# One transfer for the gate and up weights of pairs 7 to 30, and a new order of work in the first two pairs of a mixture-of-experts pass

## The reference

```python
for l in range(DEPTH):                       # DEPTH = 2
    mix = hybrid_mixer(x, mem, w_in[l], ...)
    x = layer_norm(DEEPNORM_ALPHA * x + mix, ln1_g[l], ln1_b[l])
    ffn = moe_ffn(x, w_router[l], router_bias[l], w_gate[l], w_up[l], w_down[l],
                  ws_gate[l], ws_up[l], ws_down[l])
    x = layer_norm(DEEPNORM_ALPHA * x + ffn, ln2_g[l], ln2_b[l])

def swiglu(x, wg, wu, wd):
    return (jax.nn.silu(x @ wg) * (x @ wu)) @ wd
# moe_ffn: sum over a token's 8 experts of weight * swiglu(x, w_gate[e], w_up[e], w_down[e])
#          + swiglu(x, ws_gate, ws_up, ws_down)   (the shared expert)
```

## Time and profile before

| what | value |
|---|---|
| median of 3 runs | 1187.55 us (1187.35 to 1188.29) |
| the profiled execution's own time | 1188.19 us |
| its span, first to last instruction | 1186.4 us |
| PE busy | 1148.7 us, 97% |
| DVE, ACT busy | 352.7 us, 255.3 us |
| moved by DMA | 456.49 MB, mean 385 GB/s |
| chain that ended last | PE 76%, DMA 21%, DVE 2% |
| mean granted TensorE clock | 0.996 |

### The profile page before, as it was taken

The page is one execution under the profiler, slowest core; times in us unless marked ns, Lnnn a source line. Parts: engine busy times, 40 slices in busy tenths (PEclk is TensorE's granted clock), DMA queues, the critical chain, the costliest instruction groups (busy, mean ns, idle before and its releaser), DMA issues.

```text
span 1186.4 us, 15935 instructions
## 1 busy us (share of the span) xinstructions
PE 1148.7 (97%) x6752; PEld 523.0 (44%) x6752; DVE 352.7 (30%) x1053; ACT 255.3 (22%) x511; POOL 8.4 (1%) x20
## 2 busy tenths in 40 slices
PE   8999999999999999999999999999999999999995
PEld 7774633433343333333386655333343334333331
DVE  0424722222222222222333346232222222222224
ACT  1132421222122211111112323221222122112111
POOL 0000000000000000000000000000000000000001
PEclk9999999999999999999999999999999999999998
DMA  9982599999999999999998626999999999999995
GB/s 378 421 328 113 213 415 425 428 427 426 428 426 427 428 427 428 427 427 428 413 425 360 252 80 254 412 428 428 426 429 426 428 427 426 429 426 428 426 425 224
DMA packets 39952, 456.49 MB, mean 385 GB/s; under 512 B 4416, under 2 KB 4544, under 8 KB 8256
## 3 DMA queue, kind: packets, MB, share of 16 engines
q1 hardware_dynamic: 39872, 455.38, 91.5%
HBM read 452.22 MB, written 3.15 MB: 384 GB/s over the span
## 4 chain that ended last, share of the span: by engine, by line
PE 76%; DMA 21%; DVE 2%; issue 0%; ACT 0%; POOL 0%; POOLq 0%; DVEq 0%
PE bank L705 29%; DMA slots<-in_w_gu 20%; PE bank L725 14%; PE bank L926 5%; PE bank L854 5%; PE bank L607 4%; PE bank L634 4%; PE bank L863 2%; PE bank L1052 2%; PE bank L825 1%; PE bank L713 1%; PE bank L829 1%; PE bank L873 1%; PE bank L883 1%; PE bank L959 1%; PE bank L619 1%
## 5 line engine op out<-in xcount | busy, mean ns | idle before, releaser
L705 PE MATMUL bank<-slots,front 128*64 128x512 f32 x2048 | 456.0, 595 | 13.6 <-DMA slots<-in_w_gu 13.5
L705 PEld LDWEIGHTS bank<-slots,front 128*64 128x64 f32 x2048 | 139.9, 137 | 280.8 <-issue 249.4
L725 PE MATMUL bank<-slots,r 128*32 128x512 f32 x2016 | 229.9, 595 | 1.1 <-issue 1.1
L1403 DVE SCALAR_TENSOR_TENSOR yparts<-bank,small,yparts 128x512 fp32r<-128x512 f32 x128 | 96.0, 750 | 265.4 <-ACT yparts L1086 265.4
L1086 ACT ACTIVATE yparts<-bank,small 128x512 fp32r<-128x512 f32 x128 | 87.9, 687 | 239.8 <-PE bank L725 239.8
L1395 DVE TENSOR_TENSOR high<-high,bank 128x256 f32<-128x256 f32 x64 | 26.9, 421 | 354.5 <-ACT high L1113 326.7
L725 PEld LDWEIGHTS bank<-slots,r 128*32 128x32 f32 x2016 | 59.3, 109 | 137.2 <-issue 135.7
L1113 ACT ACTIVATE high<-bank 128x256 f32<-128x256 f32 x60 | 23.0, 384 | 413.1 <-PE bank L705 413.1
L1086 ACT ACTIVATE front<-bank 128x512 f32<-128x512 f32 (+1 forms) x161 | 84.5, 580 | 88.7 <-PE bank L825 28.2
L607 PEld LDWEIGHTS bank<-selr,xparts 128*128 128x128 f32 x512 | 64.3, 188 | 45.4 <-issue 45.4
L634 PE MATMUL bank<-yparts 64*128 64x512 f32 x512 | 79.4, 421 | 1.9 <-DVE yparts L1403 1.9
(11 more groups left out here) (123 smaller groups left out, 616.6 us busy)
## 6 DMA issues: line engine op xcount, KB each, us to landing
slots<-in_w_gu SPq DMA_DIRECT2D x116, 2048.0 KB, 30.8
slots<-in_w_dn SPq DMA_DIRECT2D x58, 2048.0 KB, 27.5
slots<-in_dense SPq DMA_DIRECT2D x28, 1024.0 KB, 14.8
slots<-in_w_gu SPq DMA_DIRECT2D x24, 1024.0 KB, 9.0
slots<-in_w_dn SPq DMA_DIRECT2D x10, 1024.0 KB, 37.4
slots<-in_first SPq DMA_DIRECT2D x3, 768.0 KB, 7.0
r<-in_pool_mat SPq DMA_DIRECT2D x2, 1024.0 KB, 25.9
sdn<-in_shared_dn SPq DMA_DIRECT2D x2, 1024.0 KB, 10.0
```

The source lines that it names most:

```text
L705: m = pe.matmul(H[64 * a:64 * a + 64, :], cells[:, cell(B, k, j), a, :], GU[g][:, a, :, k, :], start=k == 0, stop=k == KD - 1)
L725: m = pe.matmul(Y[half][r0:r0 + 32, :], hT[:, kc * P + 64 * a + 32 * t:kc * P + 64 * a + 32 * t + 32], wd[:, a, kc, :], start=kc == 0, sto ...
L1403: dve.scalar_tensor_tensor(ysp[:, 1, half * 512:(half + 1) * 512], Y[half][:, :], wslot[:, b:b + 1], ysp[:, 0, half * 512:(half + 1) * 512 ...
```

## The change

There are four edits.

1. SP loads gate and up of pairs 6 to 29 in one transfer of 4 MB, issued when the pair three before has done its whole gate_up. PE waits for it before the first matmul of gate_up.
2. SP loads the first MB of pair 2's second half as soon as the first four k chunks of the second token tile's shared gate and up are read (`sgu_rd`), then half of pair 3's down weights into `xs`, then the last MB when `sh1` is full.
3. PE, ACT and DVE get a written-out order for pairs 0 and 1: gate_up of pair 1 comes before down of pair 0. On SP gate and up of pairs 3 and 4 are issued before the down weights of 3 and 4.
4. `shared_down` runs in pairs 14 to 17 and not in 26 to 29.

The diff, cut to its core:

```diff
 SPLIT = 3
+SHARED = PAIRS // 2 - 2
+WHOLE = range(6, PAIRS - 2)
+HALVES = [[q for q in range(g, PAIRS, 3) if q not in WHOLE] for g in range(3)]
...
-                def body(n, q, g, b, use, first, last):
+                def gates(n, q, g):
                     if round_ is None and q < 6:
                         for h, half in ((0, ps.h_half), (1, ps.h_full)):
                             a, m, z = h * W_CHUNK, h * W_CHUNK + W_CHUNK // 2, (h + 1) * W_CHUNK
...
+                    elif round_ is None and q in WHOLE:
+                        sp.wait_ge(ps.h_full, n - 2)
+                        sp.dma_start(slots[:, g, 0:2 * W_CHUNK], w_gu[l * PAIRS + q]).then_inc(ps.w_in[1][g], 16)
                     else:
                         sp.wait_ge(ps.h_half, n - 2)
                         load_gu(ps, l, q, g, (0,))
                         sp.wait_ge(ps.h_full, n - 2)
                         load_gu(ps, l, q, g, (1,))
+
+                def body(n, q, g, b, use, first, last):
+                    gates(n, q, g)
                     sp.wait_ge(ps.y_full, 2 * (n - 2))
                     load_dn(ps, l, q, g)
-                pairs_of_pass(base, body, 3, (lambda: load_count(sp, l)) if round_ is None else None)
+                if round_ is None:
+                    gates(base + 3, 3, 0)
+                    gates(base + 4, 4, 1)
+                    for q in (3, 4):
+                        sp.wait_ge(ps.y_full, 2 * (base + q - 2))
+                        load_dn(ps, l, q, q % 3)
+                pairs_of_pass(base, body, 5 if round_ is None else 3, (lambda: load_count(sp, l)) if round_ is None else None)
...
                 sp.dma_start(spill, xs[:].rearrange("p t d -> p (t d)")).then_inc(spill_out, 16)
-                sp.wait_ge(*full_at(l, "sh1"))
-                load_gu(main, l, 2, 2, (1,))
+                a, m, z = W_CHUNK, W_CHUNK + W_CHUNK // 2, 2 * W_CHUNK
+                sp.wait_ge(sgu_rd, l + 1)
+                sp.dma_start(slots[:, 2, a:m], w_gu[l * PAIRS + 2][:, a:m]).then_inc(third_in, 16)
                 sp.wait_ge(split_rd, 2 * l + 2)
                 sp.wait_ge(*full_at(l, "xTb3"))
                 sp.wait_ge(spill_out, 16 * l + 16)
                 sp.dma_start(xs[:].rearrange("p t d -> p (t d)"), w_dn[l * PAIRS + SPLIT][:, 0:KF * D]).then_inc(ahead_in, 16)
+                sp.wait_ge(*full_at(l, "sh1"))
+                sp.dma_start(slots[:, 2, m:z], w_gu[l * PAIRS + 2][:, m:z]).then_inc(main.w_in[1][2], 16)
...
                         if k % 4 == 0:
+                            if round_ is None and q == 2 and k:
+                                pe.wait_ge(third_in, 16 * l + 16)
                             if round_ is None and 3 <= q < 6:
                                 pe.wait_ge(quarter_in[g][k // 4], 16 * l + 16)
-                            pe.wait_ge(ps.w_in[k // 4][g], (turn * USES[g] + use) * 16 + 16)
+                            if k or (round_ is None and q in WHOLE):
+                                pe.wait_ge(ps.w_in[1][g], (turn * USES[g] + use) * 16 + 16)
+                            elif round_ is None:
+                                pe.wait_ge(ps.w_in[0][g], (turn * len(HALVES[g]) + HALVES[g].index(q)) * 16 + 16)
+                            else:
+                                pe.wait_ge(ps.w_in[0][g], (turn * USES[g] + use) * 16 + 16)
                         for a in range(2):
...
                         turn_sel(ps, q + 1)
-                        if round_ is None and q >= PAIRS - 6:
-                            i = q - (PAIRS - 6)
+                        if round_ is None and SHARED <= q < SHARED + 4:
+                            i = q - SHARED
                             shared_down(l, i // 2, i % 2)
+
+                def first_two():
+
+                    pe.wait_ge(ps.sel_rd, first_block + 2)
+                    gate_up(base, 0, 0, 0, True)
+                    for i in range(2):
+                        gather(ps, i, Y[i])
+                    shared_turn(l, 1)
+                    turn_h(base)
+                    pe.wait_ge(ps.selT_sb, base + 1)
+                    turn_sel(ps, 1)
+                    gate_up(base + 1, 1, 1, 0, False)
+                    for n, q in ((base, 0), (base + 1, 1)):
+                        if q:
+                            turn_h(n)
+                            for i in range(2):
+                                pe.wait_ge(ps.lo_rd, 2 * n - 1 + i)
+                                gather(ps, 2 + i, Y[i])
+                            combine(ps, base, 0, 0, l)
+                            combine(ps, base, 0, 1, l)
+                        pe.wait_ge(ps.w_in[2][q], turn * USES[q] * 16 + 16)
+                        pe.wait_ge(ps.hT_sb, n + 1)
+                        for half in range(2):
+                            pe.wait_ge(ps.g_sb, first_fill + KD + 2 * q + half + 1)
+                            down(q, q, half)
+                    pe.wait_ge(ps.selT_sb, base + 2)
+                    turn_sel(ps, 2)
...
-                pairs_of_pass(base, body, 0, (lambda: load_count(pe, l)) if round_ is None else None)
+                if round_ is None:
+                    first_two()
+                pairs_of_pass(base, body, 2 if round_ is None else 0, (lambda: load_count(pe, l)) if round_ is None else None)
...
                                       start=k == 0, stop=k == KD - 1)
                     if ks[-1] == KD - 1:
                         filled(l, f"sh{t}", m)
+                    elif t == 1:
+                        m.then_inc(sgu_rd, 1)
...
+                if round_ is None:
+                    for q in range(2):
+                        act.wait_ge(ps.h_full, base + q + 1)
+                        act.activation(sg[:, 0, :], H[:, 0:F], ACT.Silu).then_inc(ps.silu_rd, 1)
+                        if q:
+                            hi(base, 0)
+                        for i in range(2):
+                            g_out(1, 2 * q + i, Y[i])
+                        if q == 0:
+                            shared_turned(l, 1)
+                    hi(base + 1, 1)
+                pairs_of_pass(base, body, 2 if round_ is None else 0, (lambda: load_count(act, l)) if round_ is None else None)
...
+                if round_ is None:
+                    dve.wait_ge(ps.g_full, KD * (turn * BLOCKS + 1))
+                    build_sel(1)
+                    gated(base)
+                    turned(base)
+                    take_selT(base + 1, 1)
+                    gated(base + 1)
+                    dve.wait_ge(ps.selT_sb, base + 1)
+                    if l:
+                        dve.wait_ge(ps.lo_rd, 2 * base)
+                    lo(base, 0, 0)
+                    lo(base, 0, 1)
+                    turned(base + 1)
+                    dve.wait_ge(ps.selT_sb, base + 2)
+                    dve.wait_ge(ps.lo_rd, 2 * base + 2)
+                    lo(base + 1, 1, 0)
+                    lo(base + 1, 1, 1)
+                    take_selT(base + 2, 0)
+                pairs_of_pass(base, body, 2 if round_ is None else 0, (lambda: load_count(dve, l)) if round_ is None else None)
```

4 lines of the change are left out of this document (2 added, 2 removed).

## The result

The changed kernel takes 1192.73 us (median of 6 runs, 1190.84 to 1195.20), the kernel before 1187.92 us beside it (6 runs, 1187.35 to 1189.16): ratio 1.0044, 95% interval 1.0033 to 1.0054. It is 4.8 us slower. The forecast was 1190.5 us, 3.0 us slower than the 1187.55 that it started from. The measured time lies in the whole range of 1185.6 to 1194.0 us and 0.2 us above the 1189 to 1192.5 that the forecast's own case had. The profiled execution of the change took 1192.73 us with a span of 1190.9, so its span is 4.5 us longer than that of before. (The title counts pairs from 1: its pairs 7 to 30 are the pairs q = 6 to 29 of the text, whose gate and up go in one transfer.)

What follows compares the result with a forecast made beforehand. A pass ends by the DMA stream's length, start and losses, plus PE work behind the last landings. Per layer 1.8 - 1.6 + 1.3 = 1.5 us later, two layers 3.0: 1187.55 + 3.0 = 1190.5 us, range 1185.6 to 1194.0.

Steps and rivals of the forecast that it cites:

- the forecast's own case: Whole kernel: the summed terms hold, 1190.5 us within 1189 to 1192.5; chance 0.53.
- Edit 3, PE's part: Pairs 0 and 1: PE waits 1.9 us and 0.6 us more, entering gate_up of pair 2 some 2.5 us late.
- Edit 3, the stream's part: Opening, to pair 6's landing: late issues into empty queues make the DMA stream 1.8 us late per layer.
- Edit 2: Pair 2's early MB: worth at most 2.5 us of earlier stream per layer, used up by two empty queues.
- Edit 1, the transfer: Pairs 7 to 29: merged loads save 0.07 us a pair, 1.6 us per layer.
- the first rival: Merged loads: engines cut rows at 16 KB, so merging brings nothing; 1193.7 us; chance 0.12.
- Edit 1, the tail: Pair 29: PE must wait for all 4 MB, so the tail ends 1.3 us later per layer.
- the third rival: Tail: pair 29's gate and up land early enough, so the tail costs nothing; 1188.0 us; chance 0.2.
- Edit 4: Pairs 14 to 17: shared products, 7.6 us of PE, move no landing; PE meets the stream at pair 26.
- The second rival: Opening: the early MB's gain stays and the stream never runs dry; 1182.0 us; chance 0.13, half-way cases included.
- The fourth: Rival on merged loads: they save more than their rows show, the stream gets ahead of PE; 1178.6 us; chance 0.02.

Runs made afterwards that it cites:

- x2: The change with only the wait for the second selection matrix moved back behind gate_up of pair 0; 1190.48 us, ratio 1.0023.
- x9: The kernel before with only the early load of the first MB of pair 2's second half; 1190.54 us, ratio 1.0023.
- x4: The change with no merged 4 MB loads, halves of 2 MB from pair 6 on; 1193.84 us, ratio 1.0045.
- x6: The kernel before with only the new order for pairs 0 and 1 and SP's list to match; 1194.05 us, ratio 1.0052.
- x12: The whole change with matmuls of unused result filling PE's waits for pairs 0 and 25 to 29; 1192.48 us, ratio 1.0040.
- x11: The kernel before with merged loads for pairs 6 to 29, shared products in pairs 14 to 17, two unused matmuls ahead of pair 29's gate_up; 1186.47 us, ratio 0.9990.
- x5: The kernel before with merged loads for pairs 6 to 28 and shared products in pairs 14 to 17, pair 29 in halves; 1185.39 us, ratio 0.9980.
- x10: The kernel before with merged loads for pairs 6 to 29 and shared products in pairs 14 to 17; 1187.27 us, ratio 1.0003.
- x7: The kernel before with only the shared products moved to pairs 14 to 17; 1187.08 us, ratio 0.9999.
- x8: The kernel before with only merged loads for pairs 6 to 29, shared products still in pairs 26 to 29; 1192.06 us, ratio 1.0040.
- x3: The change with merged loads for pairs 6 to 28 only, pair 29 in two halves; 1192.69 us, ratio 1.0037.

## Why the prediction was right, and where it was not

**Edit 3, PE's part: right.** 1.76 and 0.68 us of waits for 1.9 and 0.6, gate_up of pair 2 2.7 us late for 2.5. x2 shows that the first of the two is what the stream pays for.

**Edit 3, the stream's part: this step failed in size.** "The stream is 1.5 to 2.1 us late here; I take 1.8." Down of pair 4 landed at the forecast time, but pair 6 at 211.4 instead of 209.4 to 210.0, and at down of pair 8 the stream is 2.7 and 3.3 us late. That is 2.4 us too little over both passes, where the whole sum was 1.8 us too low. The step charged the lateness of issues and the empty queue up to down of pair 4, and then took pair 6's transfer as if only its own length lay ahead of it. What failed is this sentence on pair 6: "At 7.2 to 7.8 us for the first 2 MB plus 4.9 for the others, they land at 209.4 to 210.0." It lets the load start when it is issued, at 197.36, but down of pair 5 lay ahead of it (issued at 190.28, 10.2 us to its landing) and moved until 200.4 us. Behind that landing pair 6 took 11.0 us in the first pass and 11.4 in the second, where 4 MB in a full queue take 9.7. It was issued 3.1 and 2.9 us before that landing, in the stretch of lead that x9 found dear.

Merging pair 6 brought this about. A 4 MB load goes out only when the whole slot is free, 3.5 us later than a first half would. In the ten passes with pair 6 in halves its first half was issued 6.2 us or more before the landing ahead of it and took 4.9 us, the step of a full queue. In the 18 passes with pair 6 in one transfer the lead was 2.8 to 5.1 us, and the load took 9.7 to 12.1 us, 0.7 us more than in a full queue on average: 0.9 with the opening of edit 3 and 0.6 with the old one. The kernel with edit 3 and pair 6 in halves, but pairs 7 to 29 merged, was not tried. Whether the late opening itself costs more beside merged loads stays open too: the shortest runs of x4 and x6, without them, say 1.9 to 2.0 us a pass, near the 1.8, while x12 against x11, both with them and with fillers, differ by 6.0 us, 3.0 a pass.

**Edit 2: right in its sum, wrong alone.** It was priced at nothing to 2.5 us of gain per layer, "used up by the two empty queues". Within the change that holds as far as x4 (edits 2, 3 and 4) against x6 (edit 3) shows: 1193.84 and 1194.05 us, with the same lag in their first passes. Alone it costs 0.7 to 2.1 us a pass (x9): the bytes moved earlier shorten the queue behind them.

**Edit 1, the transfer: right.** Landings of down weights in the undisturbed middle are 14.61 us apart, before 14.69: 0.08 us a pair for a forecast of 0.07, and from down of pair 8 to the last load the change wins 1.6 and 1.5 us for 1.6. In x5, which merges one pair less, it is 1.4 us a pass in the trace and 1.2 in the median. Rows of 32 KB stay whole, so the first rival is out, although its 1193.7 us is nearer to the measured time than the forecast's 1190.5; the page counts fewer packets for the same bytes:

```profile
DMA packets 33327, 456.48 MB, mean 383 GB/s; under 512 B 3680, under 2 KB 3808, under 8 KB 7520
```

against 39952 before; halving the number of rows in 48 loads of 4 MB takes 48 x 128 = 6144 away, and the trace holds 6144 packets of 32 KB, where that of before has none over 16 KB. The Trainium skill (DMA: Bandwidth & Descriptors, Why a DMA increments its semaphore by 16 and not by 1) names only rows longer than 64 KiB as ones to be cut. For rows of 32 KB the count of packets agrees.

**Edit 1, the tail: right in kind, too high in size.** 1.1 and 0.7 us in the change, 1.0 in x10's pass without a fall, 0.9 and 0.0 in x11, 0.9 and 0.3 in x12, for 1.3; x11 and x5 differ by 1.1 us for both passes together. This error offsets a part of the opening's: with the change's own 1.1 and 0.7 in place of 1.3 the forecast would have been 0.8 us lower and so farther off. That it came within 2.2 us of the median is in part luck. The wait at pair 29 is there (2.13 us), so the third rival is out.

**Edit 4: right.** No landing moved, PE meets the stream at pair 25 in the first pass and 24 in the second (forecast 26), and alone it is worth nothing that the runs can tell (x7). The forecast took it off the tail's pair before it added edit 1's wait; x8 shows what that is worth, 3.0 us a pass from the last load to the end instead of about 1.

**The second rival,** by which the early MB stays, was to be decided by down of pair 4 landing below 183.2; it landed at 184.7. **The fourth** is out with 0.08 us a pair. The section that the prediction cites for a fixed 2.0 us (the Trainium skill, DMA: Bandwidth & Descriptors, Anatomy of one DMA) gives it for transfers that GpSimd issues; this kernel's are issued by SP, and what a merge saved in the queue was 0.08 us.

**Not foreseen: the granted clock.** The forecast let PE wait at no price. A wait of about 2 us can cost another 1.4 to 1.7 us behind it. Where the next wait is for the stream, that is hidden (pair 26 of the change, x12); at pair 29 it is paid in full (x10), and at pair 0 it makes the opening later still (x3, x4, x6).

So the sum's 1.5 us a layer (1.8 - 1.6 + 1.3) is 2.2 and 2.5 us as measured (2.7 and 3.3, -1.6 and -1.5, +1.1 and +0.7).

## What to carry to other kernels

A wait that moves from behind a long step to its front is paid in full, by the engine and then again by every transfer that waits for that engine: look at the line where a wait stands before looking at the work. Where a DMA stream sets the end, a load issued earlier wins only if more loads stand behind it; price a queue by its backlog at each issue, not by its bytes alone. And where a larger transfer takes away the start on a first half, end the larger ones early enough that the compute engine finishes on halves (x5 against x10: one pair decided between 1185.4 and 1187.3 us).
